# Block inverses of an RWKV-7 recurrence on one Trainium2 core: 32x32 tiles of the array instead of 64x64

## The reference

```
def step(S, inp):
    r_t, w_t, k_t, v_t, kk_t, a_t = inp
    sa = jnp.einsum('bhvk,bhk->bhv', S, -kk_t)
    S = (S * w_t[:, :, None, :] + sa[..., None] * (kk_t * a_t)[:, :, None, :]
         + v_t[..., None] * k_t[:, :, None, :])
    return S, jnp.einsum('bhvk,bhk->bhv', S, r_t)
```

## Time and profile before

| | us |
|---|---|
| median of 3 runs | 2609.51 |
| the profiled execution: its own time | 2611.09 |
| its span | 2609.3 |
| TensorE busy | 2260.9 (87%) |
| VectorE busy | 971.6 (37%) |
| GpSimd busy | 932.6 (36%) |
| ScalarE busy | 743.0 (28%) |
| granted TensorE clock, mean over the span | 0.921 |

### The profile page before, as it was taken

One profiled execution on the slowest core, in us unless ns is written; L12 is line 12 of the kernel. 1 busy time (PEld: TensorE's weight loads), 2 busy tenths in 40 slices (PEclk: granted clock), 3 DMA queues, 4 the chain that ended last, 5 costly groups with the idle time before them and its releaser, 6 DMA issues.

```text
span 2609.3 us, 35528 instructions
## 1 busy us (share of the span) xinstructions
PE 2260.9 (87%) x15423; PEld 1833.2 (70%) x15423; DVE 971.6 (37%) x1412; ACT 743.0 (28%) x1080; POOL 932.6 (36%) x421
## 2 busy tenths in 40 slices
PE   5799999899956687786899999799999898468996
PEld 2477877588435687685677877577888687367996
DVE  2333032522486545545533022532133400635312
ACT  1412121443031111013622122432122354115433
POOL 0244434354042101102443434343444353015884
PEclk8799999899987898888999999899999898658998
DMA  9164354131000000002264354255222130013551
GB/s 329 57 208 143 121 174 153 65 115 55 12 1 2 2 3 2 2 3 97 89 201 145 121 178 154 89 169 194 95 94 87 41 135 33 0 65 107 192 186 65
DMA packets 176091, 259.66 MB, mean 100 GB/s; under 512 B 3925, under 2 KB 146275, under 8 KB 175876
## 3 DMA queue, kind: packets, MB, share of 16 engines
q1 hardware_dynamic: 172192, 250.62, 28.7%
q10 hardware_dynamic: 3748, 6.81, 0.8%
HBM read 256.37 MB, written 1.05 MB: 99 GB/s over the span
## 4 chain that ended last, share of the span: by engine, by line
PE 77%; DVE 14%; ACT 5%; issue 2%; DMA 1%; ACTq 1%; POOL 0%; DVEq 0%; POOLq 0%
PE psum L948 76%; DVE arena L1819 2%; ACT arena L661 2%; ACT u_hi L666 1%; DVE arena L1793 1%; DVE arena L1843 1%; DVE h L1603 1%; DMA arena<-k_sin 1%; ACTq L564 1%; DVE arena L1760 1%; DVE arena L1841 0%; DVE arena L1771 0%; DVE tmp L1616 0%; ACT tmp L711 0%; DVE arena L1737 0%
## 5 line engine op out<-in xcount | busy, mean ns | idle before, releaser
L2033 POOL TENSOR_TENSOR w_lo<-arena,w_hi 128x1024 fp32r<-128x1024 f32 x332 | 813.0, 2454 | 1162.9 <-ACT w_hi L629 1160.4
L948 PE MATMUL psum<-u_hi,w_hi 128*128 128x512 f32 (+1 forms) x1888 | 700.3, 371 | 84.9 <-ACT u_hi L666 49.5
L948 PE MATMUL psum<-u_hi,w_lo 128*128 128x512 f32 (+1 forms) x1888 | 689.1, 365 | 0.0
L948 PE MATMUL psum<-u_lo,w_hi 128*128 128x512 f32 (+1 forms) x1888 | 668.7, 362 | 0.0
L629 ACT ACTIVATE w_hi<-arena 128x1024 fp32r<-128x1024 f32 x332 | 348.4, 1056 | 746.2 <-PE psum L948 734.5
L948 PE MATMUL psum<-arena 64*64 64x64 f32 (+7 forms) x5828 | 440.1, 276 | 104.0 <-DVEq L1799 27.7
L948 PEld LDWEIGHTS psum<-u_hi,w_hi 128*128 128x128 f32 x1888 | 362.7, 192 | 184.4 <-issue 50.1
L948 PEld LDWEIGHTS psum<-arena 64*64 64x64 f32 (+4 forms) x5828 | 356.5, 165 | 181.3 <-issue 70.5
L948 PEld LDWEIGHTS psum<-u_hi,w_lo 128*128 128x128 f32 x1888 | 363.2, 192 | 54.1
L948 PEld LDWEIGHTS psum<-u_lo,w_hi 128*128 128x128 f32 x1888 | 357.5, 190 | 52.8 <-issue 0.2
L1573 DVE TENSOR_TENSOR tmp<-psum,tmp 128x512 f32<-128x512 f32 (+1 forms) x88 | 54.9, 624 | 593.0 <-ACT tmp L685 593.0
(11 more groups left out here) (245 smaller groups left out, 1637.9 us busy)
## 6 DMA issues: line engine op xcount, KB each, us to landing
arena<-in_ada_w SPq DMA_DIRECT2D x48, 1536.0 KB, 7.0
arena<-in_ffn_wg SPq DMA_DIRECT2D x44, 1024.0 KB, 5.4
arena<-in_ffn_wu SPq DMA_DIRECT2D x44, 1024.0 KB, 8.0
arena<-in_ffn_wd SPq DMA_DIRECT2D x20, 2048.0 KB, 8.0
arena<-in_ev_w_in SPq DMA_DIRECT2D x6, 2048.0 KB, 7.8
arena<-in_od_w_in SPq DMA_DIRECT2D x6, 2048.0 KB, 8.3
arena<-in_ffn_wd SPq DMA_DIRECT2D x4, 1024.0 KB, 5.0
arena<-in_ev_w_out SPq DMA_DIRECT2D x2, 2048.0 KB, 10.8
```

The source lines that it names most:

```text
L948: return pe.matmul(dst, w, x, start=first_, stop=last, skip_group_check=True)
L2033: pool.tensor_tensor(piece_shape(split_lo(pc), src), src, piece_shape(split_hi(pc).bitcast(F32), src), ALU.subtract).then_inc(S("lo_done"), 1)
```

## The change

`by_parts` no longer cuts a head's matrix into two tiles of 64x64. In levels 0 to 4 (m up to 16) it takes the four diagonal tiles of 32x32, since blocks of size 2m fit in them. In level 5 (m = 32) and level 6 (m = 64) it multiplies only the quarter that is new: one m x m tile in each block of 2m, with its own rows (`k`: where the contraction runs, `r`: output partitions, `n`: output columns) chosen by direction. In level 5 this is two tiles of 32x32, in level 6 one of 64x64, both off the diagonal for z or for U. What other engines do, and every wait, stays.

```
 for lv in range(LEVELS):
     m = 1 << lv
-    parts = (slice(0, 64), slice(64, P)) if lv < LEVELS - 1 else (slice(0, P),)
-
-    def by_parts(dst, w, x):
-
-        for at in parts:
-            ins = mm(dst[at, at], w[at, at], x[at, at], True, True)
+
+    def by_parts(dst, w, x, k, r, n):
+
+        for at in range(0, P, max(32, 2 * m)):
+            if m < 32:
+                ks = rs_ = ns = slice(at, at + 32)
+            else:
+                ks, rs_, ns = (slice(at + m * i, at + m * i + m) for i in (k, r, n))
+            ins = mm(dst[rs_, ns], w[ks, rs_], x[ks, ns], True, True)
         return ins
...
     z:  by_parts(bank[d][:, hh * P:(hh + 1) * P], nm[:, d, hh, 0],
-                 ident[:, :] if lv == 0 else tu[:, d, 0, hh])
+                 ident[:, :] if lv == 0 else tu[:, d, 0, hh], d, 1 - d, d)
...
-    by_parts(bank[2 + d][:, hh * P:(hh + 1) * P], tu[:, d, 1, hh], zs[:, d, hh])
+    by_parts(bank[2 + d][:, hh * P:(hh + 1) * P], tu[:, d, 1, hh], zs[:, d, hh],
+             1 - d, 1 - d, d)
...
-    ins = by_parts(bank[4 + d][:, hh * P:(hh + 1) * P], zs[:, d, hh], tu[:, d, 1, hh])
+    ins = by_parts(bank[4 + d][:, hh * P:(hh + 1) * P], zs[:, d, hh], tu[:, d, 1, hh],
+                   1 - d, d, 1 - d)
```

## The result

| | before | after |
|---|---|---|
| median, us | 2609.61 | 2691.07 (2687.25 to 2693.06, 4 runs) |
| ratio, with 95% interval | | 1.0311 [1.0293, 1.0328] |
| span of the profiled execution, us | 2609.3 | 2688.6 |
| mean granted clock | 0.921 | 0.873 |

The forecast was 2621 us, in a range up to 2690. The time is 70 us above the forecast and just outside the range. The sign and the clock's fall behind the levels were right. The failed step is the time of the levels themselves: I let them run on the times of TensorE, VectorE and ScalarE alone and put what it costs to bring the instructions at nothing.

A forecast was written before the change was run, and what follows sets the result against it. TensorE was taken to bound the kernel, holding 77% of the chain, in a three-engine ring. Levels -38 us, behind them +50, net +12 on 2611.1 gives 2623, less 1.6 for the median: 2621 us, range 2567 to 2690.

The forecast's parts named there:

- The sign: Whole kernel: slower, net +12 us against the profiled execution; chance of slower 0.56.
- the clock's fall behind the levels: Behind the levels: 48 records at half clock take 10.2 us (+4.8), denser matmuls after them +1.4; +6.2 per half.
- The failed step: Levels 0-4: four tiles at once, period 2.6 us at 2.4 GHz, 3.2 at 1.2; all levels 20 to 22 us.
- the 16 adaLN records: adaLN pieces: 16 records of 128x32 tiles, 384 columns, in 1.50 us, taken as proof of four tiles at a time.
- The second rival: Levels 0 to 4: small-tile records too slow, 0.029 us each; 2655 us, 2705 with the clock fallen; chance 0.28.
- the dearest part: Costly end of the slow-records case (2655 us, 2705 with the clock fallen), left outside the range to 2690.
- The 25 ns floor: Small-tile levels: matmuls never start less than about 25 ns apart, so 192 records cost at least 4.8 us.
- The clock inside the levels: Levels 2 to 4: granted clock near 1.0, falling to 0.5 from level 5 or 6 on.
- The first rival's sum: Clock stays at 2.4 GHz: -4.5 per half, -6.5 with transposes, mean -5.5; -44 us, 2566 us; chance 0.22.
- Levels 5 and 6: Last two levels of a half: 6.97 us becomes 5.0, -2.0 at 2.4 GHz; -0.4 at 1.2 GHz.
- The transposes: Four halves with transposes of `bk`: 1.02 us of chain, standing twice, falls into TensorE's gaps; -2.0 more each.

The follow-up runs named there:

- second run: Levels 0 to 4 as in the kernel before, levels 5 and 6 as in the changed kernel (one m x m tile per block); 2651.47 us, ratio 1.0153.
- third run: Kernel before with levels 5 and 6 on a quarter of the columns, contracted over all 2m rows of the block; 2593.08 us, ratio 0.9928.
- runs 4: Kernel before with four 32x32 tiles in levels 0 and 1 only; 2615.81 us, ratio 1.0019.
- 9: Kernel before with level 3 alone in 32x32 tiles; 2618.28 us, ratio 1.0026.
- 10: Kernel before with levels 0 to 3 in 32x32 tiles; 2638.74 us, ratio 1.0101.
- 11: Kernel before with level 6 alone by the quarter, over all 128 rows; 2603.98 us, ratio 0.9968.
- fifth run: Kernel before without matmuls and masked copies of heads 2 and 3 in levels 0 to 4, other heads in four 32x32 tiles; 2565.59 us, ratio 0.9814.
- the sixth: Kernel before without matmuls and masked copies of heads 2 and 3 in levels 0 to 4, other heads in two 64x64 tiles; 2555.98 us, ratio 0.9792.
- seventh run: Changed kernel's four 32x32 tiles in levels 0 to 4, but levels 5 and 6 on a quarter of the columns over all rows; 2645.2 us, ratio 1.0132.
- eighth run: Kernel before with three already satisfied waits written ahead of each matmul of levels 2 to 5; 2723.52 us, ratio 1.0431.

## Why the prediction was wrong, point by point

- **The failed step** is the one that took the duration of four tiles from the 16 adaLN records and let the levels run on TensorE's, VectorE's and ScalarE's times alone (period 2.6 us at 2.4 GHz, 3.2 at 1.2, "levels 20 to 22 us"). The tiles do work four at a time, even as forecast: small records start 0.009 us apart at 2.4 GHz (forecast 0.008) and 0.014 at 1.2 (59 within 0.82 us; forecast 0.0135). What I didn't carry into the sum is that 192 records are 384 instructions, one and a half packets, and a packet comes each 3.63 to 3.72 us. Between 995.34 and 1010.00 the stream delivered 512 records in 14.66 us, 0.0286 each, so 5.5 us for a level of 192, for my 2.6 to 3.2. The levels take 30.0 us in the mean where I had 22.0.
- **The second rival** was this case. It had 0.28, its price for a record was 0.029, and with the clock fallen it gave 2705 us, 14 above the measured 2691. That the number is so near is luck: 0.029 was the cost of a record on 64x64 tiles, while the small records themselves take a third to a half of it and stand still at every packet. I named the instruction fetch in its last sentence and had no row for its rate. The trace before has no stall, so it doesn't show how long a packet takes to come; it does show 121 packets and a transfer of 0.9 to 1.5 us for each, enough to make the fetch a term of the sum with a bound of its own. The range stopped at 2690 because I left out "the dearest part" of just this rival.
- **The 25 ns floor** of the Trainium skill ("TensorE: Matmul & The Clock Gate", "Wait — 56ns, not 53.3ns?") would have led to the same side for another reason. The runs speak against it for tiles on different parts of the array: the 88 records in 0.98 us start 9 ns apart in the mean. My sentence that no row settles it was a misreading, since only the mean of today's records is 0.030 us: in level 4 of the half of the earlier trace rows, from 970.71, they start in pairs 7 ns apart, and a pair each 58 ns. The same skill says of instruction fetch ("Runtime: NRT & Kernel Launch", "Instruction fetch mechanics") that blocks of 16 KiB, 256 instructions, are prefetched while the current one runs and that crossing a boundary is mostly hidden. The traces agree on the 256 and on a next block fetched while the current one runs. They disagree on "mostly hidden" once TensorE gets through a block faster than the 3.45 to 4.02 us between stalls.
- **The clock behind the levels** came as forecast: 48 records in 10.1 us (forecast 10.2) in each half, and +6.6 in all behind the levels (forecast +6.2). The second and third run show that the rows in use in levels 5 and 6 bring it about. They are not the only thing: in one half each of runs 4, 9, 10 and 11 the clock fell among the 48 records with the rows of the kernel before, or all rows, ahead of them.
- **The clock inside the levels** did not. I expected it near 1.0 in levels 2 to 4; it is 0.50 there in the half shown and 0.50 to 0.67 over the levels of a half. The fifth run, with hardly a stall, has it at 0.62 to 0.75, the sixth at 0.85 to 0.91. So the clock is lower with small tiles even when they are fed. That the emptier array is the cause is my reading; no run tests it for these levels.
- **The first rival's sum** counts level 1 twice and leaves level 4 out. With its own terms (-0.7, -1.6, -0.8, -2.0) it is -5.1 in a half, -6.1 in the mean, and some 2561 us for 2566. The clock did fall, so nothing hangs on it.
- **Levels 5 and 6**: forecast -2.0 in a half at 2.4 GHz. The third run has -2.5, with the rows that keep the clock; the second, with the rows of the change, -1.8 in the levels and then +6 or more behind them.
- **The transposes**, forecast -2.0 in each of four halves, show by half of that: halves with them became 2.8 us longer in the mean, those without 3.9 (30.5, 31.0, 29.5 and 29.9 for 27.1, 27.3, 27.7 and 27.6 with; 30.2, 30.4, 28.7 and 30.1 for 26.2, 25.0, 26.3 and 26.3 without).
- **Parts don't add up exactly.** The small tiles alone cost 41 us, on top of the few-row quarter 40, on top of the all-row quarter 52. In the last case the traces show most of the difference: behind small tiles levels 5 and 6 run at 1.2 GHz (6.9 us for 4.9 in the halves shown), so the all-row quarter gives 1.1 us in a half for 2.5, and one half lost 6.6 us behind the levels.

What stays open is what the 1.1 us ahead of a packet and the 1.4 us behind it are spent on, and what decides between a transfer of 0.9 and one of 1.4 us. The core's DMA queues move next to nothing else there (5 GB/s), so other traffic of this core isn't the reason. It isn't a limit on the rate of the queue either: in the stalled stretches it lies idle for over two of each 3.6 us. Open is also why the clock in levels 0 to 4 is lower with small tiles.

## What to carry to other kernels

Count instructions as well as columns. Cutting matmuls smaller so that more of them run side by side helps only while TensorE takes longer for 128 float32 matmul records with their weight loads (256 instructions) than a packet takes to come, 3.45 to 4.02 us here. This kernel stood at 4.33 us, and twice the instructions for the same work had no room. A short stretch may be denser: the third run has 128 records in 3.35 us at one place, without a stall. And when a product shrinks to a part of a block, halve the columns and keep the rows: zeros that are contracted cost no time (2593 us), and leaving them out took the clock away from the dense work that followed (2651 us).

## What the runs showed of the hardware that I had not expected

- Stalls of up to 2.6 us on TensorE with nothing in the profile's instructions that ends them, 256 instructions or a multiple apart, in every kernel with small tiles. They end 1.2 to 1.6 us after the end of a packet of instructions.
- A packet of instructions is fetched about 1.1 us after TensorE has begun the one before, and not earlier, even if the queue is idle.
- A float32 matmul record on 32x32 tiles each 0.009 us at 2.4 GHz.
- A wait already satisfied, as an instruction of its own between two matmuls, costs 0.07 us (eighth run, with its lower clock counted in).
- With TensorE busy 10.08 of 10.10 us on 48 records of 128x64 with 128x128 weights, the clock stayed at 1.2 GHz to the end once it had fallen ahead of them (second run), and came back at once, in seven of eight halves, when all rows had worked just ahead (seventh run).
